# A gather ring with six slots, and head 7's query weights loaded once for two groups

## What is computed

```python
h = rmsnorm(x, g_mix);  q, k, v, g, B, C, hc = split(h @ w_in)      # retention and short convolution
x = x + concat[retention(q, k, v) * silu(g), B * conv(C * hc)] @ w_out
# peer(): for every token and each of 8 heads, 16 experts out of 128 * 128
q = (x_n @ wq).reshape(tokens, 8, 2, 128)                           # x_n = rmsnorm(x, g_ffn)
s1, s2 = q[:, :, 0] . keys1, q[:, :, 1] . keys2                     # 128 scores each
top_s, eidx = top16 of (top16(s1) + top16(s2))
act  = gelu(x_n . u_tab[eidx])                                      # one row of u for each choice
x = x + sum over 8 * 16 choices of softmax(top_s) * act * v_tab[eidx]
y = rmsnorm(x, g_final)
```

## Time and profile before

| | |
|---|---|
| time, median of three runs | 2906.78 us (2905.89 to 2911.34) |
| the profiled execution: its own time, its span | 2908.83 us, 2907.0 us |
| busy share of the span: PE, DVE, ACT, POOL | 79%, 71%, 68%, 44% |
| DMA traffic | 1205.72 MB, mean 415 GB/s |
| of it by the gathers' queue (q0) | 1107.36 MB, 91.1% of 16 engines' span |
| chain of waits: DMA, PE, DVE, ACT | 47%, 27%, 12%, 10% |
| loads of `wq` into `stream` of 1 MB | 21 |

### The profile page before, as it was taken

One profiled execution on the slowest core, in us unless ns is written; L12 is line 12 of the kernel. 1 busy time (PEld: TensorE's weight loads), 2 busy tenths in 40 slices (PEclk: granted clock), 3 DMA queues, 4 the chain that ended last, 5 costly groups with the idle time before them and its releaser, 6 DMA issues.

```text
span 2907.0 us, 36104 instructions
## 1 busy us (share of the span) xinstructions
PE 2303.5 (79%) x12548; PEld 1801.2 (62%) x12548; DVE 2076.0 (71%) x5143; ACT 1971.8 (68%) x3670; POOL 1290.0 (44%) x1063
## 2 busy tenths in 40 slices
PE   9988898997786777888986878778766667666778
PEld 8877786665565556666665555555555555555566
DVE  3687888665687887777666555788978887776454
ACT  2477666777676677666667676777767666767663
POOL 0233334444443444433344354444555555555653
PEclk9999999999887889999996999888866666666669
DMA  8899999999999999999999999999999999999998
GB/s 342 320 403 408 426 420 416 411 425 425 426 426 423 426 421 424 426 426 411 424 425 399 414 417 426 426 426 426 427 426 426 427 427 424 416 425 421 427 419 340
DMA packets 182054, 1205.72 MB, mean 415 GB/s; under 512 B 21744, under 2 KB 27184, under 8 KB 43504
## 3 DMA queue, kind: packets, MB, share of 16 engines
q0 software_dynamic: 152368, 1107.36, 91.1%
q1 hardware_dynamic: 29264, 95.93, 8.3%
q10 hardware_dynamic: 240, 0.13, 0.0%
HBM read 1198.48 MB, written 4.86 MB: 414 GB/s over the span
## 4 chain that ended last, share of the span: by engine, by line
DMA 47%; PE 27%; DVE 12%; ACT 10%; issue 3%; POOL 1%; SPq 0%; DVEq 0%; ACTq 0%; POOLq 0%
DMA ring<-in_uv,idx 42%; PE expert_sum L1625 11%; DVE ring L2077 6%; ACT ring L1245 4%; DMA w_out_sb<-in_uv,idx 4%; PE mm L1508 3%; PE x_ps L1406 3%; PE mm L1311 1%; ACT weights L1241 1%; PE mm L1344 1%; PE x_ps L1311 1%; ACT L1225 1%; PE mm L1571 1%; PE x_ps L1344 1%; POOL ring L985 1%
## 5 line engine op out<-in xcount | busy, mean ns | idle before, releaser
L985 POOL DMA_INDIRECT ring<-in_uv,idx x958 | 1159.8, 1211 | 1474.7 <-PE expert_sum L1625 1263.6
L1625 PE MATMUL expert_sum<-ident_sb,ring 128*128 128x128 f32 x7472 | 1219.3, 318 | 496.3 <-ACT ring L1245 491.4
L2077 DVE CUSTOM_DVE_ANT_0 ring<-ring,xn 128x1024 f32<-128x1024 f32 x959 | 1171.1, 1224 | 591.1 <-DMA ring<-in_uv,idx 583.1
L1625 PEld LDWEIGHTS expert_sum<-ident_sb,ring 128*128 128x128 f32 x7472 | 1012.5, 164 | 770.2 <-ACT ring L1245 705.8
L1245 ACT ACTIVATE ring<-ring,weights 128x1024 f32<-128x1024 f32 x934 | 1073.1, 1149 | 30.5
L1225 ACT ACTIVATE dots<-dots 128x1 f32<-128x1 f32 x1056 | 211.8, 201 | 753.7 <-DVE dots L2077 745.8
L1241 ACT ACTIVATE weights<-dots,gate 128x1 f32<-128x1 f32 x1024 | 301.5, 294 | 38.0 <-DVE gate L2021 1.1
L1508 PE MATMUL mm<-xn_in,stream 128*128 128x416 f32 (+1 forms) x500 | 194.9, 513 | 0.0
L1625 PE MATMUL expert_sum<-ident_sb,w_out_sb 128*128 128x128 f32 x720 | 137.9, 356 | 68.3 <-ACT w_out_sb L1245 68.2
L985 POOL DMA_INDIRECT w_out_sb<-in_uv,idx x96 | 124.7, 1299 | 118.3 <-PE expert_sum L1625 106.7
L1625 PEld LDWEIGHTS expert_sum<-ident_sb,w_out_sb 128*128 128x128 f32 x720 | 112.5, 185 | 96.3 <-ACT w_out_sb L1245 94.8
(11 more groups left out here) (428 smaller groups left out, 2222.3 us busy)
## 6 DMA issues: line engine op xcount, KB each, us to landing
stream<-in_wq SPq DMA_DIRECT2D x21, 1024.0 KB
stream<-in_w_conv SPq DMA_DIRECT2D x16, 1024.0 KB
stream<-in_w_ret SPq DMA_DIRECT2D x16, 1024.0 KB
ring<-in_uv,idx POOLq DMA_INDIRECT x958
ring<-in_w_ret SPq DMA_DIRECT2D x6, 1024.0 KB, 12.3
x<-in_x SPq DMA_DIRECT2D x8, 512.0 KB, 7.8
out_y<-xn SPq DMA_DIRECT2D x8, 512.0 KB, 8.0
stream<-in_w_out SPq DMA_DIRECT2D x3, 1024.0 KB
```

Of the source, the lines that this page charges most:

```text
L985: pool.indirect_dma_start(row_of(g), None, uv, bass.IndirectOffsetOnAxis(ap=rows, axis=0)).then_inc(landed[SLOTS[g]], 16)
L1625: ins = pe.matmul(expert_sum[:, c * P:(c + 1) * P], row_of(g)[:, D + c * P:D + (c + 1) * P], ident_sb[:, :], is_transpose=True, start=Fals ...
L2077: dve.tensor_tensor_reduce(u, u, xn[:, t % 2, :], 1.0, 0.0, ALU.mult, ALU.add, dots[:, SLOTS[g]:SLOTS[g] + 1]).then_inc(dotted, 1)
```

## The change

From gather 301 (`SIX_FROM`, 43 laps of seven) the ring has six slots; slot 6 then holds the query weights of head 7, which SP loads once, when gather 300 has been added up (`load_slot_wq`). The passes of head 7 of the second and of the third group (`IN_SLOT`) read them there, and their two loads leave `STREAM`. From gather 619 (53 laps of six later) the two halves of `w_out_sb` join as slots 6 and 7, which makes eight; gathers 625 and 626 are the first in them. A semaphore that nobody waited for makes room for the new one.

```diff
--- before.py
+++ after.py
@@ -61,7 +61,8 @@
 SPLIT = 2
 
 
-RINGS = [(0, RING), (88 * RING, RING + 2)]
+SIX_FROM = 43 * RING
+RINGS = [(0, RING), (SIX_FROM, RING - 1), (SIX_FROM + 53 * (RING - 1), RING + 1)]
 
 
 def slot_of(g):
@@ -216,6 +217,7 @@
 
 SECOND_FIRST = [n for n, p in enumerate(PASSES) if p[0] == 1][0]
 LEFT_WQ = 6
+IN_SLOT = [n for n, p in enumerate(PASSES) if p[0] > 0 and p[1] == PH - 1]
 
 
 def pass_end(n):
@@ -374,7 +376,7 @@
     + [(USES[0][use_at(0, "ChB"[2 * i % 3], 2 * i, 1)][3], 0, "conv", 0, (1, i)) for i in range(KEPT_CONV // 2, CONV_UNITS // 4)]
     + [(out_at(GROUPS[1][0]) + KEPT, 0, "wout", 1, 0)]
     + [(out_at(GROUPS[j][0]) + KEPT + 2, 0, "wout", j, 1) for j in range(1, len(GROUPS))]
-    + [(p[3], 1, "wq", n, p[1]) for n, p in enumerate(PASSES) if n not in ON_CHIP])
+    + [(p[3], 1, "wq", n, p[1]) for n, p in enumerate(PASSES) if n not in ON_CHIP and n not in IN_SLOT])
 ITEM = {x[2:]: i for i, x in enumerate(STREAM)}
 HELD = ITEM["wout", 1, 0]
 ITEM["wout", 2, 0] = HELD
@@ -511,7 +513,7 @@
         squares_last = last[:, 1792:1792 + QW]
 
         def row_of(g):
-            i = SLOTS[g] - RING
+            i = SLOTS[g] - (RING if g < SIX_FROM else RING - 1)
             if i < 0:
                 return ring[:, SLOTS[g], :]
             return w_out_sb[:, 2 * i:2 * i + 2, :].rearrange("p k n -> p (k n)")
@@ -636,7 +638,7 @@
                                                           sem("par_in"), sem("g_mix_in"))
         ident_in, g_ffn_in, g_fin_in = sem("ident_in"), sem("g_ffn_in"), sem("g_fin_in")
         eps_set, root_table = sem("eps_set"), sem("root_table")
-        state_set, warmed = sem("state_set"), sem("warmed")
+        state_set, slot_wq_in = sem("state_set"), sem("slot_wq_in")
         x1_part, first_squared, xn_part = sem("x1_part"), sem("first_squared"), sem("xn_part")
         ret_half_in = sem("ret_half_in")
         first_turned, first_copied = sem("first_turned"), sem("first_copied")
@@ -877,6 +879,13 @@
                 sp.wait_ge(projected, USES_BEFORE[2] + use_at(2, "B", CONV_UNITS - 1) + 1)
                 sp.dma_start(state_s[:, :, :], ret_state).then_inc(state_in, 16)
 
+            def load_slot_wq():
+                yield SIX_FROM + 1
+                sp.wait_ge(slot_free, SIX_FROM)
+                h = PH - 1
+                sp.dma_start(ring[:, RING - 1, :].rearrange("p (b k n) -> p b k n", b=2, k=KC),
+                             wq[2 * h:2 * h + 2].rearrange("b p k n -> p b k n")).then_inc(slot_wq_in, 16)
+
             def load_x(t):
                 n = rows_of(t)
                 rows = slice(t * P, t * P + n)
@@ -934,7 +943,7 @@
                 sp.dma_start(out_ret_p, state_p[:, :, :]).then_inc(state_out, 16)
                 sp.dma_start(out_ret_s, state_s[:, :, :]).then_inc(state_out, 16)
 
-            programs = started(load_first(), load_stream(), load_consts(), load_last(),
+            programs = started(load_first(), load_stream(), load_slot_wq(), load_consts(), load_last(),
                                *[load_x_ahead(t) for t in range(2, TILES + 1)],
                                *[load_x(t) for t in range(TILES + 1)],
                                *[load_cs(t) for t in range(TILES + 1)], *[store_y(t) for t in range(TILES + 1)], store_states())
@@ -959,7 +968,9 @@
                     pool.wait_ge(chosen_first, 1)
                 elif k % TOPK == (TOPK // 2 if t == 0 and k < TOPK else 0):
                     pool.wait_ge(chosen, pick(k // TOPK, t) + 1)
-                if same_slot_before(g) is not None:
+                if g >= RINGS[2][0] and SLOTS[g] >= RING - 1 and g < RINGS[2][0] + RING + 1:
+                    pool.wait_ge(wout_done, SAMPLE + 3)
+                elif same_slot_before(g) is not None:
                     pool.wait_ge(slot_free, same_slot_before(g) + 1)
                 elif g >= RING:
                     pool.wait_ge(wout_done, SAMPLE + 3)
@@ -1260,6 +1271,9 @@
                 if kind == "wq" and j == 1:
                     pe.wait_ge(early_in, 32)
                     return turn[:, :]
+                if kind == "wq" and j in IN_SLOT:
+                    pe.wait_ge(slot_wq_in, 16)
+                    return ring[:, RING - 1, :]
                 i = ITEM[kind, j, n]
                 pe.wait_ge(stream_in[BUFFER[i]], 16 * loads_to(i))
                 return stream[:, BUFFER[i], :]
@@ -1542,9 +1556,8 @@
                 yield FIRST
                 pe.wait_ge(state_set, 1)
                 for i in range(2):
-                    ins = pe.matmul(tp[:, 1, :], state_p[:, 0, :], state_p[:, :, :].rearrange("p h c -> p (h c)"),
-                                    start=True, stop=True)
-                ins.then_inc(warmed, 1)
+                    pe.matmul(tp[:, 1, :], state_p[:, 0, :], state_p[:, :, :].rearrange("p h c -> p (h c)"),
+                              start=True, stop=True)
 
             def back(t):
                 yield end_of(t) + 1
```

## The result

The changed kernel takes 2913.44 us (median of 15 runs, 2908.99 to 2919.34), the kernel before in the same runs 2908.54 (2905.89 to 2911.34). The ratio is 1.0020, 95% interval 1.0014 to 1.0027: 5.8 us slower, at the edge of what I had called no change. 2907.1 was forecast. (The two medians differ by 4.9, and that figure stands in the expectations of e1 and e4.) Its runs also spread over 10.4 us, those of before over 5.5.

The account below looks back on a forecast made before the run. The gathers' DMA queue was taken to bound the kernel. The profiled 2908.83 us, -2.46 for the removed load and +2.79 for the lost slot, less 2.05 for that execution's distance from the median, gave 2907.1 us; range 2902 to 2914.

Parts of the forecast that it names:

- The load that goes: Head 7's weights for the third group, no longer fetched at 1983.04, free a busy DMA of one gather's time: -2.46 us.
- What moves on SP: The second group's head 7 load and the `w_ret` loads behind it go out earlier and hold nobody up: 0.
- Eight slots for nine: From gather 619: gather 981 has 11.05 us spare and one slot fewer takes about 2.46, so 0.
- the prediction's own sign of being wrong: It would be wrong altogether if the stretch behind gather 619 became thin, or gather 301 came at another time than 930.
- One slot fewer from gather 301: Gathers 301 to 625 each go out when their successor did before; the cost was put between 0.62 and 14.76, taken as +2.79 us.
- the stretches that starve now lose as much again, by the share: Thin stretches between gathers 301 and 616 repeat the loss their share of busy DMA engines shows with seven slots: 2.79 us.
- the two places named: Gathers 578 and 541, found near the floor from issue to dot product, each 0.31 us late with one slot fewer.
- The price by the floor: At gathers 541 and 578, later issue set against 5.66 us from issue to dot product: 0.31 us each, 0.62 together.
- four sizes in the text: Cost of the lost slot from gather 301: floor 0.62, share 2.79, rate 6.98, a whole gather in each of six stretches 14.76.
- The slow rival: With six slots the queue empties in all six thin stretches, a whole gather lost in each: 14.76 us, time 2919.1; chance 0.17.
- The free dips: Rival: the one late DMA engine never idles in the thin stretches, so only the floor's 0.62 counts: 2904.9 us; chance 0.27.
- The hidden removal: Rival: PE or DVE ends last around 1983, so the removed load was free: 2909.6 us; chance 0.07.

Follow-up runs that it names:

- e1: The changed kernel with head 7's weights fetched through the stream as before, ring still six then eight slots: +8.1 us against the kernel before (5.5 to 10.8).
- e4: The changed kernel with the third group's load of head 7's weights put back, unread: +6.4 us against the kernel before (3.5 to 9.3).
- e3: The kernel before without the third group's load of head 7's weights (that pass uses head 6's): -3.2 us against the kernel before (-5.8 to -0.3).
- e2: The kernel before with six slots from gather 301 to 618, then all nine, weights through the stream: +7.6 us against the kernel before (4.4 to 10.5).
- e6: The kernel before with five slots from gather 301 to 615, then nine: +63.4 us against the kernel before (59.3 to 67.5).
- e12: The kernel before with six slots from gather 301 to 510 alone: +0.3 us against the kernel before (-2.3 to 2.9).
- e5: The kernel before with six slots from gather 511 to 618, then eight: +8.4 us against the kernel before (5.5 to 11.0).
- e13: The kernel before with six slots from gather 511 to 558 alone: +4.7 us against the kernel before (2.0 to 7.3).
- e14: The kernel before with six slots from gather 560 to 619 alone: +3.2 us against the kernel before (0.6 to 5.8).
- e11: The kernel before with six slots from gather 98 to 463, slot 6 keeping a `w_ret` unit, one load less: +8.1 us against the kernel before (5.2 to 11.3).
- e10: The changed kernel with 12 idle matmuls on PE between gathers 523 and 531: +4.1 us against the kernel before (1.5 to 6.7).
- e15: The kernel before with 12 idle matmuls on PE between gathers 523 and 531: -1.7 us against the kernel before (-4.4 to 0.9).

## Why the prediction was wrong

The time fell inside the range; the change came out as +5.8 us where +0.3 was forecast. By its steps:

- *The load that goes*, -2.46: right (-2.45 and -2.53 as steps, e3).
- *What moves on SP*, 0: right in the sum, though the 2.4 us lost by 310 and regained by 341 were not foreseen.
- *Eight slots for nine*, 0: right as far as the times tell (e1 against e2, 0.5 us apart, with intervals of 3). But the prediction's own sign of being wrong shows faintly: the seven traces with eight slots lose 0.4 to 1.5 us between gathers 900 and 950, and of the nine others only e6's does. The kernel before, then the changed one:

```profile
2530.00:2570.00 40.00, 26.08 (x116) 21.08 (x117) 28.38 (x78) 24.73 (x46) 19.64 (x16) 0.61 1.02 421
2530.00:2570.00 40.00, 27.82 (x121) 22.54 (x120) 26.77 (x74) 23.68 (x45) 16.51 (x15) 0.54 1.02 407
```

- *One slot fewer from gather 301*, +2.79: wrong in size; it costs 8.1. This term failed, and with it the forecast: the step "the stretches that starve now lose as much again, by the share". Of the 2.79, 1.19 stood for the stretch at 1371, which lies in e12's six and costs nothing that shows there; the 1.60 for the four behind gather 511 stand against e5's 8.4.

Within that term the stretches around the two places named, gathers 541 to 545 and 578, were the right ones (e13, e14). For 541 the place is shown too: e13's trace has its step there. For 578 it isn't: e14's trace loses 1.2 us between 576 and 580, gains 2.0 by 585 and loses 1.0 between 585 and 600. The price by the floor, 0.31 us each, was far too low: 4.7 and 3.2. I had compared a single gather's issue, shifted by one release, with a floor of 5.66 us from an empty queue. That leaves out two things. The floor was too low: where the changed kernel starves, gather 573 is issued on POOL at 1675.67 and its dot product starts on DVE at 1682.54, 6.87 us later. The one late engine of the earlier trace rows would make the difference: a gather has landed with the last of 16 semaphore increments, and in the traces the median one comes 5.21 us behind the issue at gather 2 and 5.24 at this one, the last 5.63 and 6.84.

```profile
1675.67 0.94 POOL L996 DMA_INDIRECT ring<-in_uv,idx  x1 [2.82 <-PE expert_sum L1638]
1683.95 0.94 POOL L996 DMA_INDIRECT ring<-in_uv,idx  x1 [2.16 <-PE expert_sum L1638]
1682.54 1.23 DVE L2090 CUSTOM_DVE_ANT_0 ring<-ring,xn 128x1024 f32<-128x1024 f32 x1 [3.12 <-DMA ring<-in_uv,idx]
1694.72 1.09 PE L1638 MATMUL expert_sum<-ident_sb,ring 128*128 128x128 f32 x8
```

And a hold-up is no single gather's matter. Where nothing holds it, a slot takes some 11.9 us from issue to release (gather 576: 1683.95 to PE's 1694.72 + 1.09 = 1695.81). Six slots are 6 x 2.46 = 14.8 us of transfers, which leaves an estimated 2.9 us of hold-up before the DMA engines run dry; seven leave 5.4. The four heads of the sample's retention alone, at 3.74 us a gather, are 4 x (3.74 - 2.46) = 5.1. Where the engines ran dry already with seven, as at 1584, 1594 and 1672, the whole slot would be missing by this estimate: about 2.46 us at each, 7.4 in all, and not the small difference from a floor. That fits the 7.9 of e13 and e14, but no run shows it stretch by stretch, and the stretch at 1371, as thin with seven slots, cost nothing.

Of the four sizes in the text, 0.62, 2.79, 6.98 and 14.76, the one by the rate was near the truth, in part by luck: 3.07 of its 6.98 come from the stretches at 1083 and 1371, which cost nothing in e12, and the four behind gather 511 give 3.91. I took the one by the share because it counts idle engines. But a starved stretch shows in the rate even while the share reads full, as e11's row does (1.00 at 403 GB/s).

The slow rival had the mechanism, the queue that empties at hold-ups and is never made up; but two of its six stretches, those before gather 511, cost nothing (e12). Its loss came to 8.1 us, 3.3 gathers, just short of the 3.4 from which it was to decide. The rule of the Trainium skill's page "Perfetto Trace Analysis", section "Optimization Strategy", on repeated gaps and too few buffers agrees with e1 (+8.1) and e6 (+63.4). The free dips are out as a whole: e1 is 7.5 us over that rival's 0.62. But their reason may be why 1371 was free. In the kernel before, the last increment came 6.0 us behind the median one ahead of that dip (gather 460) and 3.3 behind it (466), in e12 3.5 and 1.7, so the late engine seems to have had work throughout; in e13 it was down to 0.6 at gather 534, ahead of the loss at 541. No run tests this. The hidden removal is out by e3.

What stays open: how much of the 4.7 us at 541 is the clock. e10's time is 1.7 us under the changed kernel's, within the noise of both; the traces' losses, 3.8 to 5.0 at a clock of 0.50 and 1.0 or less at 0.85 and 1.00, put it higher. Of the 2 us that the changed kernel's trace loses behind gather 700, 1.5 fall between 900 and 950, where e1's, with eight slots too, loses 0.6 and e2's, with nine, nothing; what makes the rest was not tried.

No version here that computes the whole layer is clearly better than the kernel before. e15, 2906.52 us against 2908.31, has an interval (-4.4 to 0.9) that lies under the changed kernel's (4.1 to 7.9) but holds 0.

## What to carry to other kernels

The depth of a ring was priced here at the hold-ups, not by the gather. As an estimate, take the cycle of a slot without a hold-up, subtract it from slots times transfer, and compare what is left with every stretch in which the releasing engine is slower than the transfers. Where the queue runs dry already, a slot less can cost a whole transfer (three stretches here fit that) or nothing (the one at 1371), so take a range and not the loss of now once more. Judge a thin stretch by its rate beside its share, and look at the granted clock of the releasing engine there, since one profiled execution can have it at the other level.

## What was not expected of the hardware

The same program point ran at either of TensorE's levels in different executions: eight transposes took 1.97 us or 1.09, the sample's retention 3.74 us a gather or 2.11, after much the same work ahead. It needs no change of the program: up to gather 559 e14's is that of the kernel before, and over the same 20 us its clock is 0.84 for 0.53. Whether this is what widens the changed kernel's runs to 10.4 us is not shown, since each kernel has one trace.
